# Output projection as seven block products from merged tiles kept in on-chip memory, with the next layer's modulation products in the down stage

## What is computed

```python
mod = silu(c) @ w_ada[l] + b_ada[l]              # sh1, sc1, g1, sh2, sc2, g2
h = rms_norm(x, norm1_g[l]) * (1 + sc1) + sh1
merged = sigmoid(gate_a) * y_a + sigmoid(gate_b) * y_b
x = x + g1 * (merged @ w_out[l])                 # the output projection
h = rms_norm(x, norm2_g[l]) * (1 + sc2) + sh2
x = x + g2 * ((silu(h @ w_gate[l]) * (h @ w_up[l])) @ w_down[l])
```

## Time and profile before

| | us |
|---|---|
| median of 3 runs | 2895.96 (2895.23 to 2896.46) |
| profiled execution, its own time | 2895.48 |
| its span on the core | 2893.6 |
| TensorE busy in the span | 2829.5 (98%) |
| VectorE / ScalarE / GpSimd busy | 2103.5 / 1223.9 / 1253.3 |

### The profile page before, as it was taken

One profiled execution on the slowest core, in us unless ns is written; L12 is line 12 of the kernel. 1 busy time (PEld: TensorE's weight loads), 2 busy tenths in 40 slices (PEclk: granted clock), 3 DMA queues, 4 the chain that ended last, 5 costly groups with the idle time before them and its releaser, 6 DMA issues.

```text
span 2893.6 us, 38026 instructions
## 1 busy us (share of the span) xinstructions
PE 2829.5 (98%) x13924; PEld 2386.9 (82%) x13924; DVE 2103.5 (73%) x2575; ACT 1223.9 (42%) x1965; POOL 1253.3 (43%) x834
## 2 busy tenths in 40 slices
PE   6999999999999999999999999999999899999998
PEld 6888889988877888888878888898888788888887
DVE  7998688865687777757668896788533878776665
ACT  3433377762242333344542335778313333233443
POOL 0354322242535555554625452223223555555454
PEclk9999999999999999999999999999999999999999
DMA  7565400224615544466635652011351345544665
GB/s 293 166 195 177 152 16 13 51 50 155 223 51 192 169 170 164 153 199 217 198 131 160 186 177 74 17 23 41 106 175 44 122 158 174 180 163 155 196 196 167
DMA packets 332745, 408.59 MB, mean 141 GB/s; under 512 B 52369, under 2 KB 242961, under 8 KB 328338
## 3 DMA queue, kind: packets, MB, share of 16 engines
q1 hardware_dynamic: 290128, 298.41, 34.0%
q10 hardware_dynamic: 42434, 107.77, 10.0%
HBM read 299.33 MB, written 104.40 MB: 140 GB/s over the span
## 4 chain that ended last, share of the span: by engine, by line
PE 86%; DVE 6%; ACT 3%; DMA 2%; POOL 1%; issue 1%; SPq 0%; ACTq 0%; DVEq 0%; POOLq 0%
PE ps L709 15%; PE ps L711 15%; PE ps L712 15%; PE ps L1775 9%; PE ps L1777 9%; PE ps L1776 9%; PE ps L1635 4%; PE ps L1616 2%; PE ps L1656 2%; PE ps L1655 2%; PE ps L1621 2%; PE ps L1620 2%; DMA raw<-in_w_b_out 1%; DVE h_lo L2581 1%; DMA ada_rows<-in_w_ada 1%
## 5 line engine op out<-in xcount | busy, mean ns | idle before, releaser
L655 POOL TENSOR_TENSOR wlo<-blocks,whi 128x512 fp32r<-128x512 f32 x288 | 430.3, 1501 | 378.0 <-ACT whi L649 375.2
L693 POOL TENSOR_TENSOR wlo<-raw,whi 128x1024 fp32r<-128x1024 f32 (+4 forms) x156 | 236.4, 1532 | 706.3 <-ACT whi L685 706.2
L649 ACT ACTIVATE whi<-blocks 128x512 fp32r<-128x512 f32 x288 | 180.4, 627 | 316.9 <-PE ps L1777 254.1
L2441 DVE TENSOR_TENSOR d_hi_lo<-blocks,d_hi_lo 128x512 fp32r<-128x512 f32 x154 | 204.3, 1330 | 140.7 <-ACT d_hi_lo L1912 140.4
L666 POOL TENSOR_TENSOR d_hi_lo<-w_pair,d_hi_lo 128x512 fp32r<-128x512 f32 x148 | 203.4, 1377 | 199.4 <-ACT d_hi_lo L1912 199.4
L709 PE MATMUL ps<-h_hi,whi 128*128 128x512 f32 x832 | 281.6, 401 | 7.0 <-DVE h_lo L2581 5.5
L711 PE MATMUL ps<-h_lo,whi 128*128 128x512 f32 x832 | 274.5, 393 | 0.0
L712 PE MATMUL ps<-h_hi,wlo 128*128 128x512 f32 x832 | 273.4, 391 | 0.0
L685 ACT ACTIVATE whi<-raw 128x1024 fp32r<-128x1024 f32 (+4 forms) x162 | 106.9, 699 | 353.0 <-PE ps L712 292.3
L1775 PE MATMUL ps<-h_hi,whi 128*128 128x512 f32 x640 | 249.5, 390 | 5.3 <-issue 3.2
L1777 PE MATMUL ps<-h_hi,wlo 128*128 128x512 f32 x640 | 249.1, 389 | 0.0
(11 more groups left out here) (338 smaller groups left out, 6888.4 us busy)
## 6 DMA issues: line engine op xcount, KB each, us to landing
blocks<-hidden_scratch SPq DMA_DIRECT2D x154, 256.0 KB, 3.7
ada_raw<-in_w_ada SPq DMA_DIRECT2D x64, 512.0 KB, 4.2
raw<-in_w_in SPq DMA_DIRECT2D x92, 256.0 KB, 4.6
w_pair<-in_w_down SPq DMA_DIRECT2D x22, 1024.0 KB, 6.2
sums_scratch<-w_pair ACTq DMA_DIRECT2D x22, 1024.0 KB, 3.9
w_pair<-sums_scratch SPq DMA_DIRECT2D x88, 256.0 KB, 3.3
blocks<-in_w_gate SPq DMA_DIRECT2D x84, 256.0 KB, 3.2
blocks<-in_w_up SPq DMA_DIRECT2D x84, 256.0 KB, 3.0
```

What stands on the lines that cost most here:

```text
L649: act.activation(block_view(whi, s), blocks[:, r, :], ACT.Copy).then_inc(block_hi.sem, 1)
L655: pool.tensor_tensor(block_view(wlo, s), blocks[:, r, :], block_view(whi, s).bitcast(F32), ALU.subtract)\
L693: last = pool.tensor_tensor(dst(wlo[:, s, :]), src(raw[:, s, :]), dst(whi[:, s, :].bitcast(F32)), ALU.subtract)
L2441: return dve.tensor_tensor(out, value, hi.bitcast(F32), ALU.subtract)
```

## The change

It brings the block scheme of the down stage to the out stage. A product has four steps there (pairs of the eight merged tiles), so a layer takes 28 steps of 12 matmuls. The merged tiles stay in on-chip memory unsplit as blocks b11 to b22 and their combinations t1 to t4 (`mg_raw`, made by VectorE behind the merge); only b11 is split at once. The w_out blocks (four pairs of 1 MB, loaded during the merge) stay on chip too, in the place of the attention mask, and VectorE forms their sums in place: `first_sums` in merge tiles 5 and 6, `second_sum` in tile 7 and behind it, `last_sum` in steps 9, 12, 16 and 20. P4's plain block has been overwritten by then and is loaded once more. Per step ScalarE copies weight and input, GpSimd makes one low part, VectorE the other, in rings of three slots; 32 evictions of 512 columns stand at fixed steps and the last four behind them. The bank of the squares' sum is one of the product's banks: TensorE reduces, per half, the sum of the first four squares and the other four square tiles singly (`summed_squares`), 20 small matmuls for 4. Both FFN weight units' low parts are made on GpSimd. The next layer's modulation blocks are loaded and reduced in layer 0's down stage, one every third step. The loops of the merge on ScalarE and VectorE are written out.

The core of the diff (indentation shortened):

```diff
+    OPAIRS = KT // 2
+    OSTEPS = 7 * OPAIRS
+    OUT_HIDDEN = {"P2": 0, "P6": 1, "P7": 2, "P5": 3, "P4": 4, "P3": 5}
+    ADA_STEPS = 6
...
+        mg_raw = sb("mg_raw", [P, 6, OPAIRS, HALF])
+        assert where[0] == zero + 96 * K
+        place(0)
+        ow_ring = sb("ow_ring", [P, 3, 2, HALF], F32R)
+        sq_late = sb("sq_late", [P, 2, HALF])
+        uo_part = sb("uo_part", [P, 4, HALF])
...
+        oh_ring = sb("oh_ring", [P, 3, 2, HALF], F32R)
+
+        place(32)
         next_raw = sb("next_raw", [P, 2, 1024])
         next_c = sb("next_c", [P, 1024])
...
+    def load_out_pair(j):
+
+        rows = w_out[l][2 * j * P:(2 * j + 2) * P, :].rearrange("(q p) n -> p q n", p=P)
+        sp.dma_start(out_pair[j].rearrange("p (q a) n -> p q (a n)", q=2), rows).then_inc(wo_loaded.sem, 16)
+
...
+        if t == 1:
+            sp.wait_ge(s_max.sem, s_max.at(l, 16 * PAIRS))
+            apart(sp)
+        if 1 <= t <= OPAIRS:
+            load_out_pair(t - 1)
...
+    sp.wait_ge(wo_loaded.sem, wo_loaded.at(l, 16 * OPAIRS))
+    for j in range(OPAIRS):
+        load_out_late(j)
+    for n in range(2):
+        sp.wait_ge(wo_lo_w.sem, wo_lo_w.at(l, 5 * OPAIRS + 2 * n + 2))
+        apart(sp)
+        up_unit(n)
+    sp.wait_ge(wo_lo_w.sem, wo_lo_w.at(l, 6 * OPAIRS + 2))
...
+        if l + 1 < DEPTH and n == 2:
+            product_done(sp, l, LAST, "S4")
+            apart(sp)
+            sp.dma_start(next_c[:, :], c_dram.broadcast_to([P, D])).then_inc(c_loaded.sem, 16)
+        if l + 1 < DEPTH and n >= 3 and n % 3 == 0 and n // 3 <= 2 * KT:
+            at = n // 3 - 1
+            load_ada(l + 1, at // KT, at % KT, ada_used.at(l, 4 * KT + at - 1), next_raw)
...
+    for n in range(OSTEPS):
+        pool.wait_ge(wo_hi.sem, wo_hi.at(l, wo_hi_number(n, 0)))
+        pool.tensor_tensor(ow_tile(n, 1), out_weight(n), ow_tile(n, 0).bitcast(F32), ALU.subtract)\
+            .then_inc(wo_lo_w.sem, 1)
+        if 18 <= n < 21:
+            add_squares(l, 1, 0, n - 17)
+        if n == 24:
+            add_squares(l, 1, 1, 1)
+        if n == 25:
+            split_lo(pool, l, U_FFN)
+        if n == 26:
+            add_squares(l, 1, 1, 2)
+    split_lo(pool, l, U_FFN + 1)
+    add_squares(l, 1, 1, 3)
...
-    for n in range(KT - 2):
-        unit_ready(pe, l, U_OUT + n)
-        wait(pe, wo_ev, l, n - 1)
...
-    for n in (KT - 2, KT - 1):
-        unit_ready(pe, l, U_OUT + n)
-        wait(pe, wo_ev, l, n - 1)
-        last_out(n, 0, range(KT)).then_inc(out_half.sem, 1)
-    last_out(KT - 2, 1, range(5))
-    mean_squares(l, 2)
-    last_out(KT - 2, 1, range(5, KT)).then_inc(unit_used.sem, 1)
-    norm_scale(l, 2)
-    last_out(KT - 1, 1, range(KT)).then_inc(unit_used.sem, 1)
...
+    def out_step(n):
+
...
+        pe.wait_ge(wo_lo_w.sem, wo_lo_w.at(l, n + 1))
+        if n < OPAIRS:
+            pe.wait_ge(mg_ready.sem, mg_ready.at(l, n + 1))
+        else:
+            pe.wait_ge(wo_lo_h.sem, wo_lo_h.at(l, n - OPAIRS + 1))
+        for m in range(4):
+            end = out_product(n, m)
+            if m == 3:
+                end.then_inc(wo_used.sem, 1)
+            elif n in (6 * OPAIRS - 1, 7 * OPAIRS - 1):
+                end.then_inc(wo_end.sem, 1)
+            if n == 25 and m == 2:
+                norm_scale(l, 2)
+
...
+        wait(pe, sq_added[half], l, (KT - 1) * (o // 2) + 3)
+        for t in range(4):
+            at = 4 * half + t
+            pe.matmul(ps[:, 6, at:at + 1], sq_sum[:, at * P:(at + 1) * P], mean_col[:, :],
+                      start=(t == 0), stop=False, skip_group_check=True)
+        for k in range(4, KT):
+            wait(pe, sq_ready[half], l, KT * (o // 2) + k + 1)
+            for t in range(4):
+                at = 4 * half + t
+                last = pe.matmul(ps[:, 6, at:at + 1], square_view(o // 2, half, k)[:, t * P:(t + 1) * P],
+                                 mean_col[:, :], start=False, stop=(k == KT - 1), skip_group_check=True)
+                if t == 2 and k == KT - 1:
+                    last.then_inc(sq_added[half].sem, 1)
+            last.then_inc((sq_mm if k == KT - 1 else sq_added[half]).sem, 1)
...
+    for n in range(OSTEPS):
+        out_step(n)
+        if n == 24:
+            pe.wait_ge(wo_ev.sem, wo_ev.at(l, 32))
+            summed_squares(l, 2)
...
+            if k == 0:
+                pe.wait_ge(wo_ev.sem, wo_ev.at(l, 33 + 2 * w_i + t))
...
-    mean_squares(l, 3)
+    wait(pe, std_ready, l, 3)
+    pe.wait_ge(wo_ev.sem, wo_ev.at(l, 36))
+    summed_squares(l, 3)
...
+        if n < OPAIRS:
+            act.wait_ge(wo_loaded.sem, wo_loaded.at(l, 16 * OPAIRS))
+            wait(act, unit_used, l, U_MERGE + KT - 1 + n // 2)
+        elif n < OPAIRS + 3:
+            wait(act, unit_used, l, U_MERGE + KT)
+        else:
+            act.wait_ge(wo_used.sem, wo_used.at(l, n - 2))
...
+        copy(ow_tile(n, 0), out_weight(n)).then_inc(wo_hi.sem, 1)
+        if n >= OPAIRS:
+            copy(oh_tile(n, 0), out_hidden(n)).then_inc(wo_hi.sem, 1)
...
+    table(ACT.Sqrt)
+    wait(act, unit_used, l, U_MERGE + KT)
...
+    for n in range(2, 26):
+        wo_hi_part(n)
+        if n in (6, 7):
+            for m in (2 * (n - 6), 2 * (n - 6) + 1):
+                act.wait_ge(wo_used.sem, wo_used.at(l, OPAIRS))
+                copy(uo_part[:, m, :], ps[:, m, :]).then_inc(uo_copied.sem, 1)
+        if 16 <= n < 20:
+            out_square(0, n - 16)
+        if 23 <= n < 26:
+            out_square(1, n - 23)
+        if n == 24:
+            split_hi(act, l, U_FFN)
+    for k in range(4, KT):
+        out_square(0, k)
+    wo_hi_part(26)
     norm_std(l, 2)
-    split_hi(act, l, U_FFN)
...
+    wo_hi_part(27)
     split_hi(act, l, U_FFN + 1)
...
+    hidden_hi(l, 2, 0)
+    hidden_hi(l, 2, 1)
+    out_square(1, 3)
+    hidden_hi(l, 2, 2)
...
+    out_square(1, 6)
+    out_square(1, 7)
...
+        dve.tensor_tensor(m_ab[:, 0, :], pair(4 * j), gl[:, 0, :], ALU.mult).then_inc(mg_step.sem, 1)
+        dve.tensor_tensor(m_ab[:, 1, :], pair(4 * j + 2), gl[:, 1, :], ALU.mult).then_inc(mg_free.sem, 1)
+        if t == KT - 1:
+            for p in range(2):
+                second_sum(p)
+        dve.wait_ge(mg_step.sem, mg_step.at(l, 2 * t + 1))
+        wait(dve, mg_free, l, t + 1)
...
+            both = mg_raw[:, 0:6:5, q, :]
+        dve.tensor_tensor(both, m_ab[:, 0, :].rearrange("p (h n) -> p h n", h=2),
+                          m_ab[:, 1, :].rearrange("p (h n) -> p h n", h=2), ALU.add).then_inc(mg_step.sem, 1)
+        dve.wait_ge(mg_step.sem, mg_step.at(l, 2 * t + 2))
...
+        dve.tensor_tensor(t3, b22, b12, ALU.subtract).then_inc(mg_comb.sem, 1)
+        dve.wait_ge(mg_comb.sem, mg_comb.at(l, 4 * q + 1))
+        dve.tensor_tensor(t2, b22, t1_, ALU.subtract).then_inc(mg_comb.sem, 1)
+        dve.wait_ge(mg_comb.sem, mg_comb.at(l, 4 * q + 3))
+        dve.tensor_tensor(t4, b21, t2, ALU.subtract).then_inc(mg_comb.sem, 1)
...
+        dve.wait_ge(wo_lo_w.sem, wo_lo_w.at(l, j + 1))
+        dve.wait_ge(wo_sum.sem, wo_sum.at(l, 2 * j + 1))
+        dve.tensor_tensor(a11, a22, a11, ALU.subtract).then_inc(wo_sum.sem, 1)
...
+    for t in range(KT):
+        merge_tile(t)
+        if t in (5, 6):
+            for j in range(2):
+                first_sums(2 * (t - 5) + j)
+    for j in range(2, OPAIRS):
+        second_sum(j)
...
+        dve.wait_ge(wo_hi.sem, wo_hi.at(l, wo_hi_number(n, 1)))
+        lo_of(oh_tile(n, 1), out_hidden(n), oh_tile(n, 0)).then_inc(wo_lo_h.sem, 1)
...
+        for m in (2 * (n % 2), 2 * (n % 2) + 1):
+            if n in (10, 11):
+                part_added(m, 2)
+            elif n in (14, 15):
+                out_done_to(3)
+                add_out(m, 0, ps[:, m, :])
+            elif n in (18, 19):
+                part_added(m, 4)
+            elif n in (20, 21):
+                out_evicted(17 + m)
+                add_out(4 + m, 1, uo_part[:, m, :])
+            elif n in (22, 23):
+                out_done_to(5)
+                out_evicted(21 + m)
+                add_out(4 + m, 1, ps[:, m, :])
+        if n in (12, 13, 16, 17):
+            if n == 12:
+                for back in x_back:
+                    wait(dve, back, l, 16)
+            part_out({12: 0, 13: 1, 16: 2, 17: 3}[n])
...
+        out_hidden_low(n)
+        if n in (9, 12, 16, 20):
+            last_sum((9, 12, 16, 20).index(n))
+        out_evictions(n)
+    for m in range(4):
+        out_last_eviction(6, m)
+    out_hidden_low(OSTEPS - 2)
     norm_inverse(l, 2)
-    wait(dve, unit_used, l, U_OUT + KT - 1)
-    last_out(KT - 2, 1)
+    out_hidden_low(OSTEPS - 1)
     wait(dve, a2_ready, l, 1)
     dve.tensor_tensor(sh_step[:, :], mod[:, 3, 4:KT], mod[:, 3, 0:4], ALU.subtract).then_inc(sh_ready.sem, 1)
+    dve.wait_ge(wo_lo_w.sem, wo_lo_w.at(l, 6 * OPAIRS + 1))
     hidden_scaled(l, 2, 0)
...
-    weight_lo(l, U_FFN + 1)
-    for k in range(3, 6):
+    for m in range(2):
+        out_last_eviction(7, m)
+    hidden_lo(l, 2, 3)
```

(7 more changed lines are left out.)

294 lines of the change are left out of this document (158 added, 136 removed).

## The result

The changed kernel took 2925.32 us (median of four runs, 2919.21 to 2929.07), the kernel before beside it 2896.21 (2895.23 to 2897.43): a ratio of 1.0098, 95% interval 1.0079 to 1.0118. It is slower by 1%, outside the forecast's range. A repeat gave 1.0093 (1.0078 to 1.0108). An interval of a ratio is 3 to 6 us to either side, so two kernels of my own are told apart by their times only if they differ by more, and otherwise by their traces.

A forecast was written before the change was run, and what follows sets the result against it. TensorE, busy 98% of the span, was taken as the bound. Terms -21.8 + 13.0 + 4.2 + 1.8 + 0.5 = -2.3 us gave 2893.2 against the profiled 2895.48, stated as 2893.7 for the median; range 2885.5 to 2904.

The forecast's parts named there:

- the small matmuls added: Sums of squares, both halves and layers: 64 more small matmuls on TensorE at 0.2025 us each, nothing hiding them, +13.0 us.
- The signs put on record: Traces: 40 small matmuls a layer at 0.2 us; wrong if TensorE idles under 0.5 or over 6 us per out stage.
- the modulation products: Layer 0's down stage: moved loads and products hidden except a late start at step 4, +0.5 us (0 to 2.5).
- Rival (C): Down stage can't take the moved loads: each of 16 delays a step by 0.55 us, +8.8, 2902.5; chance 0.07.
- the steady steps: Out stage, steps 10 to 23: VectorE's overrun covered by 2.7 us of slack, cost nothing; upper bound 2.9 a layer.
- the matmuls removed: Out projection: 336 matmuls of 512 columns a layer for 384, 0.2274 us each, -21.8 us over two layers.
- P6's wait: Opening of the out stage's second product: TensorE waits 2.1 us for VectorE's low part, twice, +4.2 (wait bounds 0, 4.2).
- the hand-over: Out stage to FFN: two waits for evictions, 1.8 us for 0.8 before; +1.8 in all (-1.6 to +4).
- the two rules weighed there: VectorE beside GpSimd at the second product's opening: alternation, wait 2.1 us, taken; whole-instruction blocking, wait 4.2, kept as bound.
- Rival (B): VectorE bounds the out stage by mutual exclusion: 4.2 wait at P6, 2.9 a layer in steps 10-23; +7.7, 2903.7; chance 0.17.

The follow-up runs named there:

- s_twenty: Kernel before with each sum of squares in front of the FFN reduced by 20 small fp32 matmuls for 4: 2925.58 us, ratio 1.0087.
- m_loads: Changed kernel with the moved modulation loads but without the 16 products on VectorE: 2920.47 us, ratio 1.0069.
- c_all: Changed kernel with all moves at once, among them later loads, small matmuls in five spaced groups, second half's squares summed by GpSimd: 2910.01 us, ratio 1.0036.
- c_best2: c_best with square root and reciprocal ahead of step 27's parts, row scales one column block later, sh_step at step 8, FFN's first bank freed sooner: 2897.7 us, ratio 0.9994.
- f_pairs: Changed kernel with the first half's last four square tiles added in pairs by VectorE, 12 small matmuls for 20: 2918.67 us, ratio 1.0067.
- s_fewer: Changed kernel with 11 small matmuls per sum of squares for 20, part of the sums left out: 2907.47 us, ratio 1.0028.
- c_best: Changed kernel with the gaining parts together: later loads, reordered VectorE sums, first half's squares paired, second half's summed by GpSimd: 2900.35 us, ratio 1.0002.
- c_best3: c_best2 with GpSimd's three additions of squares at steps 18, 20 and 22 for 18, 19 and 20: 2899.44 us, ratio 0.9998.
- s_spread: Changed kernel with each sum's 20 small matmuls in five groups of four between big ones, first half's row scales later: 2924.6 us, ratio 1.0096.

## Why the forecast was wrong

**The step that failed: "the small matmuls added".** It priced 64 at 0.2025 us, from a row of four, as if five such rows in a row cost five times as much. The sum's largest unknown was taken as its surest term: the rows that I had read showed the small ones only four at a time, and I gave no upper bound. The trace of the kernel before had a longer row, which I did not look at: eight in a row for the squares of another norm, ahead of the merge, and the clock falls right behind them, in both layers (at 329.3 and 1742.5), with TensorE busy:

```profile
327.47 1.93 PE L1540 MATMUL ps<-columns,lat_sq 128*128 128x1 f32 x16
329.25 1.13 PE L709 MATMUL ps<-h_hi,whi 128*128 128x512 f32 x2
...
329.30:332.80 3.50, 3.50 (x10) 2.72 (x11) 3.37 (x8) 0.00 (x0) 0.00 (x0) 0.51 0.15 33
```

Measured: the four places in the kernel before with 16 more each cost 25 us (s_twenty) for 13. In the changed kernel the small matmuls added and the half-rate stretch behind them took 11.9 us a layer for the 6.5 of the sum, 5.4 more in each layer. In layer 0 that is 0.6 and 1.9 beyond 4.05 on the small ones and the rest on the big ones behind them, at 0.43 for 0.227. None of the rivals had it. The signs put on record point the same way: the small ones are 40 a layer, but take 0.23 and 0.30 us each in layer 0's two rows for the 0.2 foreseen, while TensorE's idle time in the out stages, 4.05 and 4.41 us, lies inside the 0.5 to 6 foreseen. "Stays at the full granted clock", read in the earlier trace rows, was a state of the stage before, and I carried it over to a stage that works differently.

**The step "the modulation products" was mis-sized**: +0.5 (0 to 2.5) for 9.0 in the profile. I saw the place, SP behind the last FFN product at step 2, and took 1.5 us of lateness less 1 of slack; but ScalarE waited 5.4 us for the input block of step 4, and TensorE 3.52, with the clock at 0.50 for 3.4 us behind it. The share of the products was set at nothing; VectorE's row of the stage rose from 139.8 to 161.2 us, and waits behind it of 2.5 us in all followed (the longest 1.41, at 1350), which are gone in m_loads. Rival (C) had this outcome and its size, 8.8, at a chance of 0.07, but by luck, with another mechanism: a cost per load, where it was one wait at the start and then VectorE.

**The step "the steady steps" was mis-sized**: 0, with an upper bound of 2.9 a layer; measured 2.51 and 2.54, all at step 21. (The slack that it was weighed against is 5.44 - 2.54 = 2.9 by its own rows, not 2.7.) The reason I gave for nothing was that evictions take 0.68 to 0.74 "alike beside GpSimd". That was read from the median in the earlier trace rows, where the same row's longest is 1834 ns. In the changed kernel the source view of the eviction shows both kinds:

```profile
L3110 DVE SCALAR_TENSOR_TENSOR x_sb<-ps,mod,x_sb x32: 730/738/747, 763.1 to 2248.6; 128x512 f32<-128x512 f32 x32
L3110 DVE SCALAR_TENSOR_TENSOR x_sb<-uo_part,mod,x_sb x24: 737/1768/1782, 757.2 to 2218.2; 128x512 f32<-128x512 f32 x24
```

With one input in PSUM none of the 32 is held up; with two SBUF inputs its median is 1768 ns.

**Right**: the matmuls removed (the changed kernel's first 48, before any wait, take 10.88 us, 0.2267 a piece); P6's wait, 2.1 forecast, 1.54 and 1.87 measured, at the place named; the hand-over, two waits of about 1 us for evictions, 1.05 and 1.06 (0.42 and 1.10 in layer 1). Of the two rules weighed there, alternation was the better estimate for the opening. For a single instruction the page's rule fits: the Trainium skill, "SBUF — State Buffer", section "Who interferes with whom", has the second one wait for the whole of the first, and sh_step, 0.15 us by itself, took 2.34 beside a GpSimd instruction of 2.62 and ended with it.

Rival (B), VectorE as the bound, is half true: its price in steps 10 to 23 was right, that at P6 not.

The sum set right, against the profiled run: -2.3, -0.8 for P6 (3.4 for 4.2), +5.1 for step 21, +8.5 for the down stage, +0.5 for the hand-over (2.3 for 1.8) make +11.0; the clock's 10.8 make 21.8, and 1.9 of the 23.7 stay open. The median of the runs lies 6 us above the profiled one. What differs between two traces of the same kernel is the clock behind waits of 2.5 to 5 us. The mean granted clock of the runs goes with their times: 0.990 at 2919.21 and 0.987 at 2929.07 in the first four, 0.993 at 2901.37 and 0.987 at 2915.15 in c_all. As 0.001 of it costs up to 2.9 us, the clock is enough for the spread; where the runs without a trace lost it was not shown.

## What to carry to other kernels

A price taken from four of a thing isn't one for twenty in a row on an engine whose clock depends on what it is given: when a change puts small matmuls in a row, ask what the clock does, look in the trace that you have for a longer row than the one you price, and keep GpSimd or VectorE on the sum where they have the time. A gain in work is worth only what the chains around it leave: in c_best2 21.8 us of matmuls are gone for 3.2 of small ones (16 more than before, both layers together). Waits of 5.0 us in each layer and the lower clock leave 3.9 us of that, and the stretch between the two out stages, above all the down stage with the moved products, takes 4.5 back: a time that can't be told from that of before. And read the longest duration of a source row beside the median before calling an instruction undisturbed.

## What the runs showed of the hardware

TensorE's granted clock fell to 0.50 (1.2 GHz) behind, or still within, every row of 20 fp32 matmuls of one column, in all 44 places of the traces kept; four of them are s_twenty's and four the changed kernel's. It was back at 1.00 between 3.4 and 10.2 us after it had fallen. In the first halves of these two kernels TensorE had waited nowhere for 8 us before the row; before the second halves it had had one or two short waits (0.42 to 1.10 us, 2 to 6 us ahead). Shorter rows did it in some places: 12 in one of two in f_pairs, 11 in three of four in s_fewer, and the eight ahead of the merge in both layers of the kernel before and in 31 of the 38 places of all traces. Twelve with waits of 0.34 and 0.62 us between the groups did it in all six places of c_best, c_best2 and c_best3. Four small ones didn't do it in the out stages of the kernel before; five groups of four with 0.68 us of big ones between did it in none of four places in s_spread, and in one of two in c_all, where a wait of 1.2 us stood ahead of both. The Trainium skill, "TensorE: Matmul & The Clock Gate", section "What's actually happening", has the gate set by how busy TensorE has been recently. In the places with the row of 20 the profile's busy time was 100% and the clock fell all the same, so that figure doesn't show the fall coming.
